# The second MLP product as twenty block products per half instead of seven half products

## The reference

```
h = rms_norm(x, g_mlp) * (1.0 + scale2) + shift2
ff = jnp.square(jax.nn.relu(h @ w_ff1)) @ w_ff2      # w_ff1 1024 x 4096, w_ff2 4096 x 1024
x = x + gate2 * ff
y = rms_norm(x, g_final)
```

## Time and profile before

| | us |
|---|---|
| runs | 1443.58, 1447.25, 1447.31; median 1447.25 |
| profiled execution: span | 1441.9 |
| profiled execution: device time | not given apart from the runs above |
| median of the runs less the span | 5.4 |
| TensorE busy | 1402.4 (97%) |
| VectorE, ScalarE, GpSimd busy | 809.9 (56%), 591.7 (41%), 479.5 (33%) |
| granted TensorE clock, mean | 0.995 of 2.4 GHz |
| DMA | 232.35 MB, 161 GB/s |

### The profile page before, as it was taken

How to read it: one execution, slowest core, us unless ns; L and a number is a source line. 1 busy time by engine, 2 the same in 40 slices (tenths; PEclk the granted TensorE clock), 3 DMA queues, 4 the chain that set the end, 5 groups by cost and what they waited for, 6 DMA issues and landing times.

```text
span 1441.9 us, 18527 instructions
## 1 busy us (share of the span) xinstructions
PE 1402.4 (97%) x7594; PEld 1188.8 (82%) x7594; DVE 809.9 (56%) x756; ACT 591.7 (41%) x709; POOL 479.5 (33%) x275
## 2 busy tenths in 40 slices
PE   4999999999999989999999999999999999999997
PEld 2777777888888778888888888888888888888886
DVE  5967668794338994444453345352756433344575
ACT  6667888566135532232222222232232222433241
POOL 0011111137002655474545555432232222232131
PEclk9999999999999999999999999999999999999998
DMA  9344311203602234343334333479997444445542
GB/s 371 152 153 170 135 61 37 73 23 95 234 0 88 88 125 160 114 154 114 122 143 145 119 119 126 172 258 389 391 384 297 146 146 146 161 177 204 204 160 88
DMA packets 75411, 232.35 MB, mean 161 GB/s; under 512 B 5696, under 2 KB 9920, under 8 KB 66368
## 3 DMA queue, kind: packets, MB, share of 16 engines
q1 hardware_dynamic: 75328, 231.17, 43.5%
HBM read 166.14 MB, written 65.01 MB: 160 GB/s over the span
## 4 chain that ended last, share of the span: by engine, by line
PE 50%; issue 3%; POOL 1%; DVE 1%; ACT 0%; POOLq 0%; ACTq 0%
PE bank L981 17%; PE bank L982 17%; PE bank L983 16%; POOL w_lo L2339 1%; DVE x L2151 0%; DVE w_raw L2102 0%; POOL x L2361 0%; ACT hin_hi L1527 0%; ACT w_hi L1515 0%; DVE x L2123 0%; POOL w_s L2315 0%; PE bank L1038 0%; POOL w_lo L2331 0%; PE bank L1031 0%; POOLq L2369 0%
## 5 line engine op out<-in xcount | busy, mean ns | idle before, releaser
L981 PE MATMUL bank<-hin_hi,w_lo 128*128 128x512 f32 (+1 forms) x896 | 302.4, 337 | 1.4 <-DVE hin_lo L2107 1.4
L982 PE MATMUL bank<-hin_lo,w_hi 128*128 128x512 f32 (+1 forms) x896 | 301.7, 337 | 0.0
L983 PE MATMUL bank<-hin_hi,w_hi 128*128 128x512 f32 (+1 forms) x896 | 301.1, 336 | 0.0
L2107 DVE TENSOR_TENSOR hin_lo<-hin,hin_hi 128x3072 fp32r<-128x3072 f32 x28 | 140.9, 5031 | 209.1 <-ACT hin_hi L1527 209.1
L2339 POOL TENSOR_TENSOR w_lo<-w_raw,w_hi 128x2048 fp32r<-128x2048 f32 x28 | 129.6, 4628 | 329.9 <-ACT w_hi L1515 328.4
L981 PEld LDWEIGHTS bank<-hin_hi,w_lo 128*128 128x128 f32 x896 | 170.1, 190 | 20.4 <-issue 2.3
L983 PEld LDWEIGHTS bank<-hin_hi,w_hi 128*128 128x128 f32 x896 | 169.9, 190 | 18.0
L982 PEld LDWEIGHTS bank<-hin_lo,w_hi 128*128 128x128 f32 x896 | 170.1, 190 | 17.7 <-issue 0.2
L1515 ACT ACTIVATE w_hi<-w_raw 128x2048 fp32r<-128x2048 f32 x28 | 53.6, 1916 | 287.6 <-PE bank L983 181.7
L2331 POOL TENSOR_TENSOR w_lo<-w_raw,w_hi 128x512 fp32r<-128x512 f32 x51 | 73.5, 1441 | 208.5 <-ACT w_hi L1461 208.5
L1470 ACT ACTIVATE hid<-bank 128x768 f32<-128x768 f32 (+2 forms) x68 | 52.5, 772 | 162.7 <-PE bank L983 155.3
(11 more groups left out here) (273 smaller groups left out, 3171.1 us busy)
## 6 DMA issues: line engine op xcount, KB each, us to landing
hin<-hid_all SPq DMA_DIRECT2D x28, 1536.0 KB, 6.6
hid_all<-hid SPq DMA_DIRECT2D x105, 384.0 KB, 2.5
w_raw<-in_w_ff SPq DMA_DIRECT2D x36, 1024.0 KB, 8.9
w_raw<-in_w_ff SPq DMA_DIRECT2D x68, 256.0 KB, 2.9
mod_raw<-in_w_mod SPq DMA_DIRECT2D x16, 1024.0 KB, 5.1
x<-in_xT SPq DMA_DIRECT2D x5, 2048.0 KB, 14.1
w_sums<-w_raw SPq DMA_DIRECT2D x8, 1024.0 KB, 15.3
w_raw<-w_sums SPq DMA_DIRECT2D x8, 1024.0 KB, 10.1
```

Source lines behind the costliest of these rows:

```text
L981: pe.matmul(out, w_lo, v_hi, start=first, stop=False, skip_group_check=True)
L982: pe.matmul(out, w_hi, v_lo, start=False, stop=False, skip_group_check=True)
L983: return pe.matmul(out, w_hi, v_hi, start=False, stop=last, skip_group_check=True)
L2107: dve.tensor_tensor(hin_lo[n % 3][:].rearrange("p t n -> p (t n)"), hin[n % 3][:].rearrange("p t n -> p (t n)"), hin_hi[n % 3][:].rearrang ...
```

## The change

The tokens are cut into three chunks of 512, the output features into two halves, the contracted 4096 into two halves of 2048, and each of those into four blocks of 512. For each contraction half twenty products of sums of blocks replace the 24 plain ones (3 x 4 x 2), so there are 40 steps (`NS`) of 4 x 128 contracted features, 4 x 128 outputs and 512 tokens. A step is four banks of 4 x 3 matmuls, 48 of 512 columns. Products in `RIGHT` go to banks 0 to 3, the others to banks 4 to 7; some start on a bank that still holds the sum of earlier ones.

- **TensorE** waits for both halves of a step's lo parts, then fills bank 0 to its end, bank 1, and so on (`product`, `BY_BANK` holds all steps). Ahead of banks 0 and 2 it waits until the last product of that side has been copied or added out of the pair (`bank_emptied`).
- **ScalarE** splits weights and tokens in two pieces of 128x1024 each; both wait for the end of step n-2 (`piece_end`). In the first contraction half it copies five blocks of 128x2048 into the accumulators (`block_copies`) and one more; once per half it moves a weight sum (`move_b0`). At the end it squares five blocks of 128x2048 and scales nine tiles.
- **GpSimd** makes `w2_lo` in two instructions of 128x1024 per step, and at the end `fin_adds` (128x2048, 128x1024, 128x512, twice) and nine output tiles.
- **VectorE** makes `tok_lo` in two instructions of 128x1024 per step; 17 weight sums (`weight_sum`) and 8 token sums (`token_add`) of 128x2048 per half; `block_adds`, 13 blocks in the first half and 20 in the second, each two instructions of 128x1024 from PSUM onto the accumulator in SBUF (or four of 128x512 with the gate, for the products in `FINAL`); six `conv_block` of four instructions of 128x512, which turn an accumulator into gate x sum + residual (loaded again from `x_mid`).
- **SyncE** loads one token form of 1 MB for each step but that of product 14, which takes a sum made in `k14` (one load per half), and eight weight blocks of 1 MB per half. No sum is stored.
- **First MLP product**: `hid_out` forms six sums or differences of 512 columns for a whole job in place of four of 768, `store_form` writes nine tiles of 512 columns in place of seven of 768; the short job forms two, with two tiles loaded again first (`reload_rest`).
- **Tail**: the last block is chunk 0's second feature half, 512 columns wide; its banks are added, squared and summed one by one; the last outputs are 512 columns wide.

The diff, cut to its core (the lists that set the order, TensorE's, ScalarE's, VectorE's and GpSimd's loops):

```diff
+NP = 20
+SEQ = (7, 6, 10, 9, 5, 2, 8, 3, 4, 19, 1, 17, 16, 13, 18, 15, 12, 14, 11, 0)
...
+FRESH = (7, 6, 5, 2, 16, 12)
...
+ADDED = (
+    {9: ((1, 0),), 3: ((0, 0),), 8: ((0, 1), (1, 1)), 17: ((2, 0),), 16: ((2, 1),), 13: ((2, 0),), 18: ((1, 0),),
+     15: ((1, 1),), 12: ((2, 1),), 14: ((2, 0),), 11: ((0, 0),), 0: ((0, 1),)},
+    {6: ((0, 1),), 10: ((0, 0), (1, 0), (2, 0)), 9: ((1, 0), (2, 0)), 2: ((1, 1),), 3: ((0, 0),),
+     8: ((0, 1), (1, 1)), 1: ((2, 1),), 17: ((2, 0),), 16: ((2, 1),), 13: ((2, 0),), 18: ((1, 0),), 15: ((1, 1),),
+     12: ((2, 1),), 14: ((2, 0),), 11: ((0, 0),), 0: ((0, 1),)})
+COPIED = {6: ((0, 1),), 10: ((0, 0), (1, 0)), 2: ((1, 1),), 1: ((2, 1),)}
+FINAL = (18, 15, 12, 14, 11, 0)
+CONV_AT = {10: (1, 0), 13: (1, 1), 14: (2, 1), 15: (2, 0), 17: (0, 0), 18: (0, 1)}
...
+SAME_NEXT = (11, 12, 13, 14, 16, 17, 18)
...
-        def ff2_step(n):
+        def bank_part(n, b, tiles):
+
+            fresh = SEQ[n % NP] in FRESH
+            w = slice(b * P, (b + 1) * P)
+            for t in tiles:
+                w_hi = w2_hi[n % 2][:, t, w]
+                w_lo = w2_lo[SLOT[SEQ[n % NP]]][:, t, w]
+                m = three_more(bank_of(n, b), w_hi, w_lo, tok_hi[n % 2][:, t], token_lo_of(n)[:, t],
+                               fresh and t == 0, t == GF - 1)
+            return m
+
+        def bank_emptied(n, b):
+
+            if b % 2:
+                return
+            m = same_bank(n)
+            if m is None:
+                if SEQ[n] in RIGHT:
+                    pe.wait_ge(ff1_copy, 4 * NJ)
+                    pe.wait_ge(hid_step, hid_at(NJ - 1, C22))
+                else:
+                    pe.wait_ge(hid_step, hid_at(NJ - 1, C12))
+                return
+            if copied(m):
+                pe.wait_ge(ff2_copy, copies_to(m))
+            if added(m):
+                pe.wait_ge(ff2_add, adds_to(m, b // 2))
+
+        def split_in(n, p):
+
+            pe.wait_ge(w2_lo_done, 2 * n + p + 1)
+            pe.wait_ge(tok_lo_done, 2 * n + p + 1)
+
+        def product(n):
+
+            if n % NP in BY_BANK:
+                split_in(n, 0)
+                split_in(n, 1)
+                for b in range(4):
+                    bank_emptied(n, b)
+                    m = bank_part(n, b, range(GF))
+                    if n == NS - 1:
+                        m.then_inc(final_mm, 1)
+                    elif b > 0:
+                        m.then_inc(ff2_mm, 1)
+                    if n == NS - 2 and b == 1:
+                        fin_spread(0)
+                    elif n == NS - 1 and b == 0:
+                        fin_columns(1)
+                    elif n == NS - 1 and b == 1:
+                        fin_spread(1)
+                return
...
+        def fin_spread(at):
+
+            pe.wait_ge(rstd_done, 2 * NN + at + 1)
+            pe.matmul(bank[at][:], ones[:], fin_diag[:], start=True, stop=True).then_inc(norm_bc, 1)
+
+        for n in range(NS):
+            if n == NS - 2:
+                fin_columns(0)
+            product(n)
...
+        def split_w2_hi(n, p):
+
...
+                act.wait_ge(ff2_mm, piece_end(n - 2, p))
...
+        split_w2_hi(1, 0)
+        split_tok_hi(1, 0)
+        for s in range(NS):
+            h, i = half_of(s)
...
+            if s + 1 < NS:
+                split_w2_hi(s + 1, 1)
+                split_tok_hi(s + 1, 1)
...
+            if s + 2 < NS:
+                split_w2_hi(s + 2, 0)
+                split_tok_hi(s + 2, 0)
...
+        for s in range(NS):
+            h, i = half_of(s)
+            if i == 8:
+                token_add(h, "a14")
+            if s > 0 and added_later(s - 1):
+                block_adds(s - 1, 1)
+            if s + 1 < NS:
+                tok_split_lo(s + 1, 0)
+            if s > 0 and not added_later(s - 1):
+                block_adds(s - 1, 0)
+                block_adds(s - 1, 1)
+            if s + 1 < NS:
+                tok_split_lo(s + 1, 1)
+            for name in {1: ("b0a",), 2: ("b0b", "v"), 3: ("b2", "b3"), 5: ("b19",), 6: ("b4",), 7: ("b1",), 8: ("b17",),
+                         11: ("b13",), 13: ("v15", "b12"), 14: ("b14a", "b14b"), 16: ("b11",)}.get(i, ()):
+                weight_sum(h, name)
+            if s == NP - 1:
+                weight_sum(1, "u")
+                weight_sum(1, "b6")
+            if i in (8, 9, 10, 11, 12, 14, 16):
+                token_add(h, {8: "a1", 9: "a17", 10: "a16", 11: "a13", 12: "a18", 14: "a12", 16: "a11"}[i])
+            if h and i in CONV_AT:
+                conv_block(CONV_AT[i])
+            if s == NS - 2:
+                fin_diagonal(0)
+            if s < NS - 1 and added_later(s):
+                block_adds(s, 0)
+            if s == NS - 2:
+                for v, k in ((1, 0), (1, 1), (1, 2), (1, 3), (0, 0)):
+                    final_tile(0, v, k)
...
+            of = slice(2 * p, 2 * p + 2)
+            pool.tensor_tensor(w2_lo[SLOT[f]][:, of], src[:, of], w2_hi[n % 2][:, of], ALU.subtract
+                               ).then_inc(w2_lo_done, 1)
...
+        for s in range(NS):
+            if s + 1 < NS:
+                w2_split_lo(s + 1, 0)
+                w2_split_lo(s + 1, 1)
+            if s == NP + 16:
+                fin_adds(0, (1, 0), (1, 1))
+            elif s == NP + 18:
+                fin_adds(1, (2, 1), (2, 0))
+                fin_tiles(0, (1, 0))
...
```

More of the change, by code:

```diff
@@ new lines, in kind_of, with steps_of, hid_at, stores_of @@
+def kind_of(q):
+    return JOBS[q][0] % 8 // GF
+def steps_of(q):
+    both = (U2, C11, B11, C22, B22, C12, B12)
+    _, c0, c1 = JOBS[q]
+    if c0:
+        return both + (F19, FZ)
+    if c1 == CH:
+        return both + (F3, F5, F2, F15)
+    return both + ((F0, F4, F7, F6, F9, FR) if kind_of(q) else (F3, F19, F5, FZ, F2, F15))
+def hid_at(q, step):
+    return sum(len(steps_of(i)) for i in range(q)) + steps_of(q).index(step) + 1
+def stores_of(q):
+    _, c0, c1 = JOBS[q]
+    return (7, 8) if c0 else range(7) if c1 == CH else range(NST)
@@ new lines, in added, with copied, adds_to, copies_to @@
+def added(n):
+    h, i = half_of(n)
+    return ADDED[h].get(SEQ[i], ())
+def copied(n):
+    return COPIED.get(SEQ[n], ()) if n < NP else ()
+def adds_to(n, e):
+    return 2 * sum(len(added(m)) for m in range(n)) + (e + 1) * len(added(n))
+def copies_to(n):
+    return sum(len(copied(m)) for m in range(n + 1)) + (n >= SEQ.index(9))
+def same_bank(n):
+    side = SEQ[n % NP] in RIGHT
+    return next((m for m in range(n - 1, -1, -1) if (SEQ[m % NP] in RIGHT) == side and (added(m) or copied(m))), None)
@@ new lines, in same_slot, with ring_at, of_ring, sum_at @@
+def same_slot(n):
+    at = SLOT[SEQ[n % NP]]
+    return next((m for m in range(n - 1, -1, -1) if SLOT[SEQ[m % NP]] == at), None)
+def ring_at(n):
+    h, i = half_of(n)
+    return len(RING) * h + RING.index(SEQ[i])
+def of_ring(r):
+    h, at = divmod(r, len(RING))
+    return NP * h + SEQ.index(RING[at])
+def sum_at(h, name):
+    return len(SUMS) * h + SUMS.index(name) + 1
+def token_sum_at(h, name):
+    return len(TOKEN_SUMS) * h + TOKEN_SUMS.index(name) + 1
+def added_later(n):
+    return n % NP in SAME_NEXT or n == NP - 1
@@ new lines, in build_encoder @@
+    w2_lo = [place(f"w2_lo{i}", UW, F32R, unit[u]) for i, u in enumerate(SLOT_UNIT)]
+    w2_hi = [place(f"w2_hi{i}", UW, F32R, unit[u]) for i, u in enumerate((14, 1))]
+    RING_UNIT = (3, 17, 5)
+    tok = [place(f"tok{i}", UW, F32, unit[u]) for i, u in enumerate(RING_UNIT)]
+    tok_lo = [place(f"tok_lo{i}", UW, F32R, unit[u]) for i, u in enumerate(RING_UNIT)]
+    tok_hi = [place(f"tok_hi{i}", UW, F32R, unit[u]) for i, u in enumerate((16, 2))]
+    k14 = place("k14", UW, F32, unit[19])
+    k1 = place("k1", UW, F32, unit[20])
@@ L336, in build_encoder @@
     ld_wo = [sem(f"ld_wo{i}") for i in range(3)]
[L337 to L338 removed]
+    st_y = sem("st_y")
     const_set = sem("const_set")
@@ L2050, in out_of, with halves, split, pieces @@
                 return ps[:, 2 * CH * buf + c0:2 * CH * buf + c1]
-            slot, at = hid, NHID * q
+            def halves(lo_row):
+                return hidq[:, lo_row:lo_row + 2, CH:HTOK]
+            def split(i):
+                return form[i][:].rearrange("p (a b) -> p a b", a=2)
+            def pieces(row):
+                return hidq[:, row, 0:CH].rearrange("p (a b) -> p a b", a=2)
+            def stored_before(j):
+                if q:
+                    after(dve, st_hid[j], stored(j, q - 1))
+            h11, h12, h21, h22 = (hidq[:, i, 0:CH] for i in range(4))
             if step == U2:
@@ L2130, in fin_add, with flat @@
[L2130 to L2143 removed]
+        def flat(t):
+            return t[:].rearrange("p t n -> p (t n)")
@@ new lines, in conv_block, with fin_diagonal @@
+        def conv_block(b):
+            n = max(m for m in range(NP, NS) if b in added(m) and SEQ[m - NP] not in FINAL)
+            dve.wait_ge(ff2_add, adds_to(n, 1))
+            dve.wait_ge(ld_x[CHUNK_OF[b[0]]], 48 if b == (1, 0) else 64)
```

(16 more changed lines are left out.)

1140 lines of the change are left out of this document (672 added, 468 removed).

## The result

The changed kernel takes **1518.17 us** (median of 4 runs, 1515.31 to 1519.61) against 1446.01 (1443.58 to 1447.31) for the kernel before, measured beside it: ratio 1.0497, 95% interval 1.0477 to 1.0518. The forecast was 1506, range 1438 to 1540.

A forecast was written before the change was run, and what follows sets the result against it. TensorE was taken to bound the second product's stage: 437.8 of matmuls, 86.9 of waits and 2.8 of norm matmuls make 527.5 against 472.4, 55 us more; with 4 for the tail, 1447.25 + 59 = 1506 us, range 1438 to 1540.

The forecast's parts named there:

- Step of 10.94 us, 437.8 in all: Second product: 40 products of 48 matmuls of 512 columns at 0.228 us, against 467.0 us before.
- Turns between VectorE and GpSimd: GpSimd's instructions and VectorE's with two SBUF inputs take turns, first asker first; VectorE's with one PSUM input are never held.
- Waits of 86.9: Second product's stage: TensorE's waits in a walk of 40 steps through four queues sum to 86.9 us.
- fifth and tenth products: Each half, plus the sixth of the second: adds or a14 stand ahead of the splits, 15.9 us of waits.
- the first norm's diagonal: Last product but one: TensorE's fin_spread(0) waits for fin_diagonal(0) behind conv_block and fin_adds(1), 12.3 us.
- Second half, steps 11 to 17: TensorE waits 7.0, 10.3, 5.9, 8.2 and 1.8 us, together 33.2, behind VectorE's sums, conv, adds and GpSimd's turns.
- Clock, kept out of the sum: TensorE's clock falling after long waits: 1.6 us each, 13 us for eight, 27 for all; counted only in the range.
- rival 3: TensorE's clock falls at every long wait: 1519 to 1533 us, up to 1540 with GpSimd's upper price; chance 0.14.
- First MLP product "at nothing": Added subtractions, stores and reload are covered, no net cost; uncovered 5 us in all, the reload 3 us.
- Tail 4 more: After TensorE's last product: wider last block makes 11.4 us of 7.3, 4 us more, bounds 2 and 6.
- Rival 1 (faster): Turns fall better, stage nears 437.8 us, TensorE's waits under some 28 us: 1424 to 1443 us; chance 0.20.
- Rival 4: The change doesn't do what it says: with nothing gained or lost, 1447 us; chance 0.03.

The follow-up runs named there:

- run 1: Changed kernel with GpSimd's weight splits cut to 32 columns, leaving out the low part of the second product's weights: 1464.07 us.
- run 3: Changed kernel with all 80 weight splits of the second product moved from GpSimd to VectorE: 1492.15 us.
- run 8: Changed kernel with run 3, run 5, run 6 and banks filled one by one only where the next product needs them, by pieces elsewhere: 1457.55 us.
- run 9: Changed kernel with the first two final norms' additions of squares moved from GpSimd to VectorE and the first norm's diagonal formed earlier: 1511.23 us.
- run 2: Changed kernel, first MLP product: G5 of job 0 formed right after G3, job 6's A11 and A21 loaded ahead of job 4's stores: 1511.37 us.
- run 5: Run 2's edits on the changed kernel, plus the kept form stored first and job 6's A12 and A22 loaded ahead of four stores: 1502.95 us.
- run 6: Changed kernel with the first final norm's spread moved into the last product, after its first bank: 1518.58 us.
- run 10: Run 8 with run 9's edit, two residual blocks moved to emptier steps and the first norm's spread at its old place: 1450.40 us.
- run 11: As run 10, but with the first norm's spread in the last product: 1445.26 us.
- run 12: Run 11 with two banks emptied ahead of sums at steps 13, 14, 17, 18 and the second norm spread one bank later: 1447.55 us, ratio 1.0016.

## Why the prediction came out as it did

Direction and range held; the sum lay 12 us low. In the spans it is 14.7 (73.8 grown against 59): three errors, of which two, in the waits and in the clock, nearly cancel. That they did is luck. The medians show less because they grew by 72.2 and the median before, 1447.25 when I carried it, is 1446.01 with a fourth run.

- **Step of 10.94 us, 437.8 in all:** right in every run (438.0 to 438.6 by spacing with the norm matmuls, 228 ns between full-speed matmuls).
- **Turns between VectorE and GpSimd:** right, and runs 1, 3, 8 and 9 show it. Splits of 1.21 us took 2.55, GpSimd's 2.94; bank additions from PSUM stayed at 1.21.
- **Waits of 86.9:** too many by 22; measured 64.8. Place by place, forecast and measured (the spacing less 0.23 at each): ahead of the second step 9.0, 5.2 (2.6 in runs 2, 5, 6 and 9); first half where the banks are needed again 15.1, 13.3; fifth and tenth products 15.9, 11.5; second half 33.2, 22.7; the first norm's diagonal 12.3, 8.1; the other norm matmuls 1.4, 3.9. The term most off is "Second half, steps 11 to 17: 7.0, 10.3, 5.9, 8.2, 1.8". They measured 6.2, 9.8, 1.0, 3.6 and 2.2: the first two and the last within 0.8, and behind the long one the queues had caught up more than in my walk. Why the walk left too much of it is not settled.
- **Clock, kept out of the sum:** this was the wrong choice. It cost 23.9 us in the stage, within the 13 to 27 of rival 3. With 64.8 for the waits, it brings the stage to 527.1, where the forecast had 527.5 for other reasons. Rival 3's range (1519 to 1533) just missed 1518.17: it added the clock to waits that were too long by 22, and had nothing for the first product's 14. The Trainium skill's warning (TensorE: Matmul & The Clock Gate, HAM oscillation) that waits can throttle the engine again and again is borne out by this trace: 0.94 over the stage, and one spell of half speed after another. The 1533 that I worked out by it was 15 too high.
- **First MLP product "at nothing":** the step that made the 12 us. I named covers (VectorE half idle, 29 us a job) and bounds of 5 and 3 us, looking at how much work is added. The loss came from two places in the order: a bank copy behind G5 behind token work (a pause of 7.1 us), and weights behind stores in SyncE's queue (7.0 us). The product took 14.0 us more, of which the order of the queues gave back 9.4 (run 5). "Issued a step or more ahead" was checked for the second product's loads and not for the first's.
- **Tail 4 more:** measured 5.1.
- **Rival 1 (faster)** asked for waits under 28 us. Only runs 10 to 12, with the edits above together, reach it (19.6 to 21.6), and they land near the time of before: the first product keeps 4 to 7 us of its loss, the clock takes 5 to 8 in the stage, and the end behind the last product takes 4 to 7 more than before (11.4).
- **Rival 4** fell: the matmuls are as the code says. No wait of TensorE ended on a token or weight load in the second stage.

## What to carry to other kernels

Count as one resource the instructions of VectorE and GpSimd that read two operands from SBUF: add their times before giving work to the second engine, and if the sum comes near the time of the step, keep it on the faster one. When fewer matmuls leave a step shorter, what stands between "buffer free" and "operand ready" doesn't shrink with it, and each longer pause that results (over some 3 us here) is paid twice, in itself and in clock. For a queue that is said to cost nothing, look at what stands ahead of the one entry that somebody waits for, not at its load.

## What the runs showed of the hardware beyond that

- **The price of a fall hardly grows with the pause.** I listed the 133 pauses of about 1 us and more ahead of product matmuls of this stage, in the thirteen traces of the changed kernel and its edits (spacing of starts; those right behind a norm's spread left out), with the time lost to half-speed spacings behind each, up to the next pause. Behind the 33 of 1.0 to 2.2 us 0.1 at most was lost but four times (0.3 to 0.6). Behind the 68 of over 3.1, all but four lost 1.3 to 3.1, mostly 1.6 or 1.7: in the changed kernel 1.7 behind 3.4, 1.8 behind 6.4, 2.1 behind 10.0. The 32 between 2.3 and 3.1 went either way: twenty lost 1.5 to 1.9 and eleven 0.1 (in the changed kernel 0.1 behind one of 2.5 and 1.7 behind another). So, as an estimate from these prices, bringing a pause from 3.5 us to 2 is worth 3 us, the second half of it in clock; half speed fell from 23.9 to 5.5 us between the changed kernel and run 12.
- **A busy engine that does nothing.** VectorE's busy time in the stage fell by 110 us when another engine's work was removed (run 1). A busy share of 69% on the page said nothing of that; the mean of a group against the same width with a PSUM input (2.55 against 1.21) did.
- **Held for a whole chain.** In run 8 a group of four short VectorE instructions took 7.5 us longer (10.18 instead of 2.7) beside three GpSimd additions in a row of 9.4 us together; that is more than the four themselves take.
